# Two-layer diffusion trunk on one core: weight split four units deep, ada loads on the ScalarE queue, a residual scan, and diagonal blocks moved in small pieces

## The reference, cut to what matters

```python
mod = silu(c) @ w_ada + b_ada                       # shift, scale and gate, for latent and context
p = (rmsnorm(x, norm_w) * (1 + sc) + sh) @ w_in     # 2048 -> 8224 columns
# attention: two softmaxes per head, a = p0 - lam * p1
# delta rule, per head and direction, in chunks of C tokens (g cumulated in the chunk):
m = tril_strict(k_beta @ k.T * decay) + eye         # unit triangular
u, w = solve(m, v * beta), solve(m, k_beta * exp(g))
v_new = u - w @ state
o = (q * exp(g)) @ state + (q @ k.T * decay) @ v_new
state = state * exp(g_last) + k_end.T @ v_new
x = x + gt * (concat(y_a, y_b) @ w_out)
```

## Time and profile before

| | us |
|---|---|
| timed runs | 2801.6, 2818.62, 2807.7 |
| median | 2807.7 |
| profiled execution, span from first to last instruction | 2805.5 |
| PE busy | 2441.5 |
| DVE busy | 1479.5 |
| ACT busy | 840.5 |
| POOL busy | 335.5 |

### The profile page before, as it was taken

How to read it: one execution, slowest core, us unless ns; L and a number is a source line. 1 busy time by engine, 2 the same in 40 slices (tenths; PEclk the granted TensorE clock), 3 DMA queues, 4 the chain that set the end, 5 groups by cost and what they waited for, 6 DMA issues and landing times. The chain is left out here.

```text
span 2805.5 us, 41589 instructions
## 1 busy us (share of the span) xinstructions
PE 2441.5 (87%) x15126; PEld 2006.7 (72%) x15126; DVE 1479.5 (53%) x2582; ACT 840.5 (30%) x1415; POOL 335.5 (12%) x685
## 2 busy tenths in 40 slices
PE   6799999999898989897898798988889898987776
PEld 2377778777776868685776476868777686866775
DVE  1345556473737373745433746475656656565535
ACT  3433232323223232323111533223232323223223
POOL 0001011111102020201100002020111202021100
PEclk9999999999999999998998699999999999998888
DMA  8945352626253544434334244443243444333433
GB/s 324 355 113 153 83 152 62 167 70 173 70 152 91 140 104 126 110 102 147 109 104 151 81 108 119 103 107 101 77 110 78 123 106 107 95 92 112 125 110 110
DMA packets 580888, 345.00 MB, mean 123 GB/s; under 512 B 45090, under 2 KB 544966, under 8 KB 579990
## 3 DMA queue, kind: packets, MB, share of 16 engines
q1 hardware_dynamic: 553430, 300.38, 38.7%
q10 hardware_dynamic: 27120, 42.02, 4.7%
q0 software_dynamic: 208, 0.72, 0.1%
HBM read 312.07 MB, written 31.00 MB: 122 GB/s over the span
## 5 line engine op out<-in xcount | busy, mean ns | idle before, releaser
L1604 PE MATMUL ps<-h_hi,w_hi 128*128 128x512 f32 (+1 forms) x2080 | 846.7, 407 | 49.2 <-DVE w_lo L972 38.1
L1605 PE MATMUL ps<-h_lo,w_hi 128*128 128x512 f32 (+1 forms) x2080 | 780.5, 375 | 0.0
L1606 PE MATMUL ps<-h_hi,w_lo 128*128 128x512 f32 (+1 forms) x2080 | 779.6, 375 | 0.0
L972 DVE TENSOR_TENSOR w_lo<-w_raw,w_hi 128x1024 fp32r<-128x1024 f32 (+1 forms) x332 | 405.4, 1222 | 329.7 <-ACT w_hi L569 270.0
L1604 PEld LDWEIGHTS ps<-h_hi,w_hi 128*128 128x128 f32 x2080 | 407.6, 196 | 166.5 <-issue 64.4
L569 ACT CAST w_hi<-w_raw 128x1024 fp32r<-128x1024 f32 (+1 forms) x332 | 340.6, 1029 | 522.0 <-PE ps L1606 197.5
L1606 PEld LDWEIGHTS ps<-h_hi,w_lo 128*128 128x128 f32 x2080 | 407.1, 196 | 70.0
L1605 PEld LDWEIGHTS ps<-h_lo,w_hi 128*128 128x128 f32 x2080 | 409.4, 197 | 47.9
L1457 POOL TENSOR_SCALAR small<-small 128x4 f32<-128x4 f32 (+3 forms) x51 | 14.0, 274 | 2056.5 <-DVE small L1260 1018.1
L1854 PE MATMUL ps<-h_hi,w_hi 128*128 128x512 f32 (+1 forms) x448 | 169.7, 379 | 56.7 <-DVE w_lo L972 56.7
L972 DVE TENSOR_TENSOR arena<-arena,ps 128x512 f32<-128x512 f32 x160 | 104.1, 684 | 129.5 <-PE ps L1686 128.6
(11 more groups left out here) (187 smaller groups left out, 3164.0 us busy)
## 6 DMA issues: line engine op xcount, KB each, us to landing
w_raw<-in_w_in SPq DMA_DIRECT2D x260, 512.0 KB, 4.6
ada_raw<-in_w_ada SPq DMA_DIRECT2D x148, 512.0 KB, 5.4
w_raw<-in_w_out SPq DMA_DIRECT2D x64, 448.0 KB, 3.7
w_raw<-in_w_ada SPq DMA_DIRECT2D x44, 512.0 KB, 7.0
arena<-decay_rows ACTq DMA_DIRECT2D x16, 512.0 KB, 5.4
m_chunks<-arena SPq DMA_DIRECT2D x16, 512.0 KB, 5.5
arena<-s_chunks SPq DMA_DIRECT2D x16, 512.0 KB, 3.9
x_channel_major<-arena ACTq DMA_DIRECT2D x1, 4096.0 KB, 17.2
```

What stands on the lines that cost most here:

```text
L972: return V.tensor_tensor(o, a, b, op)
L1604: mm(o, w_hi[:, s, k], h_hi[:, kt, t0:], start=kt == 0, stop=False)
L1605: mm(o, w_hi[:, s, k], h_lo[:, kt, t0:], start=False, stop=False)
L1606: last = mm(o, w_lo[:, s, k], h_hi[:, kt, t0:], start=False, stop=kt == KT - 1)
```

## The change

It does six things.

- w_raw gets two buffers, w_hi and w_lo four each; the splits run three units ahead (LEAD) instead of one.
- The ada loads inside the heads move from SP's queue to ACT's: after the copy of product k, ACT asks for both halves of k+1; those of k = 0 in slot 30.
- w is not formed any more. From the second step on, PE multiplies the keys by the state (ks_mul), DVE forms the residual v - exp(g) (k state) (residual; the table row is negated once per layer), and v_mul takes one product per direction. POOL no longer forms k_grow, ACT no longer copies w.
- The diagonal blocks move as eight pieces of 16 partitions each way; the DRAM images hold blocks only, and POOL clears inv_T in SBUF instead of a DRAM image of zeros being written once.
- A block of 16 is solved as two halves of 8, both in the same instructions, and joined by two small products on DVE and POOL.
- Slots move: substitution 14 to 17 (was 15 to 19), turns of the inverse 22 and 23 (24, 25), merge levels from 24 (27), v products at 37, 43, 49, 55 (42, 46, 50, 54), output of the head one slot later. The start-up ring of ada loads has seven buffers instead of six.

```diff
+RAW = 2
+SPLIT = 4
+LEAD = SPLIT - 1
+RING = RAW + 5
...
+    def blocks_of(t, b):
+        return t.rearrange("(x b) (r n) -> b r x n", b=NB, n=BLK)[b]
...
-        w_raw = sb("w_raw", [P, 4, HALF, P])
-        w_hi = sb("w_hi", [P, 2, HALF, P], F32R)
-        w_lo = sb("w_lo", [P, 2, HALF, P], F32R)
+        w_raw = sb("w_raw", [P, RAW, HALF, P])
+        w_hi = sb("w_hi", [P, SPLIT, HALF, P], F32R)
+        w_lo = sb("w_lo", [P, SPLIT, HALF, P], F32R)
...
         def substitution(k, d):
+            m, s_ = diagonal_halves(blk_m, d), diagonal_halves(blk_s, d)
+            t = blk_t[d * NT * NB:(d + 1) * NT * NB, 0:2 * SUB * SUB].rearrange("p (h r n) -> p h r n", h=2, r=SUB)
             if d == 0:
-                up = BLK - 1 - k
-                return m[:, 0:up, up:up + 1], s_[:, up:up + 1, up:], s_[:, 0:up, up:], t[:, 0:up, up:]
+                up = SUB - 1 - k
+                return m[:, :, 0:up, up:up+1], s_[:, :, up:up+1, up:], s_[:, :, 0:up, up:], t[:, :, 0:up, up:]
...
+        def corner_product(eng, own, d, out_, a, b):
+            terms = blk_t[d * NT * NB:(d + 1) * NT * NB].rearrange("p (r n k) -> p r n k", r=SUB, n=SUB)
+            own.done(eng.tensor_tensor(terms, a.unsqueeze(2).to_broadcast(terms.shape),
+                                       b.rearrange("p k n -> p n k").unsqueeze(1).to_broadcast(terms.shape), ALU.mult))
+            if d:
+                own.done(eng.tensor_reduce(out_, terms, AX, ALU.add))
+                return
+            for k in (4, 2):
+                own.done(eng.tensor_tensor(terms[:, :, :, 0:k], terms[:, :, :, 0:k], terms[:, :, :, k:2 * k], ALU.add))
+            own.done(eng.tensor_tensor(out_.unsqueeze(3), terms[:, :, :, 0:1], terms[:, :, :, 1:2], ALU.add))
+
+        def join_halves(eng, own, d):
+            i, j = (0, 1) if d == 0 else (1, 0)
+            spare = corner(blk_m, d, j, i)
+            corner_product(eng, own, d, spare, corner(blk_m, d, i, j), corner(blk_s, d, j, j))
+            corner_product(eng, own, d, corner(blk_m, d, i, j), corner(blk_s, d, i, i), spare)
+            own.done(eng.tensor_scalar(corner(blk_s, d, i, j), corner(blk_m, d, i, j), -1.0, None, ALU.mult))
...
+        SUBST, SOLVED, LEVEL0 = 14, 22, 24
+        V_SLOT = (37, 43, 49, 55)
...
             def w_unit(i, u, source, tiles=HALF):
-                s = u % 4
+                s = u % RAW
...
-                    sp.wait_ge(w_split, i * UNITS + (u - 3))
+                    sp.wait_ge(w_split, i * UNITS + (u - RAW + 1))
...
                 def blocks_to_partitions(i):
-                    sp.dma_start(chunk_rows(m_dram), m_T.rearrange("p x c d -> p (x c) d")).then_inc(blocks_out, 16)
-                    sp.wait_ge(blocks_out, nth(layer, i, -1, 16, 16))
-                    sp.dma_start(sub(blk_m), diagonal_blocks(m_dram)).then_inc(blocks_in, 16)
+                    for b in range(NB):
+                        rows = slice(b * BLK, (b + 1) * BLK)
+                        sp.dma_start(blocks_of(m_dram, b),
+                                     m_T.rearrange("p x c d -> p (x c) d")[rows, :, rows]).then_inc(blocks_out, 16)
+                    sp.wait_ge(blocks_out, nth(layer, i, -1, 16 * NB, 16 * NB))
+                    sp.dma_start(blk_m, m_dram).then_inc(blocks_in, 16)
...
-                        if fill and k == 8:
+                        if fill and k == 7:
                             blocks_to_partitions(i)
-                        if fill and k == 10:
+                        if fill and k == 9:
                             blocks_back(i)
...
-                        if k >= 10 and k - 10 < ADA_IN[layer]:
-                            for hf in range(2):
-                                ada_unit(layer, i, k - 10, hf)
...
             def split_hi(i, u, tiles=HALF):
-                s = u % 4
-                act.wait_ge(w_loaded[s], i * (16 * UNITS // 4) + 16 * (u // 4 + 1))
-                need(act, w_used, i * UNITS + (u - 1))
-                nc.scalar.copy(w_hi[:, u % 2, 0:tiles], w_raw[:, s, 0:tiles]).then_inc(w_hi_ready, 1)
+                s = u % RAW
+                act.wait_ge(w_loaded[s], i * (16 * UNITS // RAW) + 16 * (u // RAW + 1))
+                need(act, w_used, i * UNITS + (u - SPLIT + 1))
+                nc.scalar.copy(w_hi[:, u % SPLIT, 0:tiles], w_raw[:, s, 0:tiles]).then_inc(w_hi_ready, 1)
...
                     def ada(k):
                         ada_copy(i * ADA_IN[layer] + (ada_before(layer) + k + 1))
+                        if k + 1 < ADA_IN[layer]:
+                            ada_load(k + 1)
+
+                    def ada_load(k):
+                        lay, firstb = ada_block(layer, k)
+                        for hf in range(2):
+                            act.dma_start(ada_raw[:, hf], w_ada[lay].rearrange("(k p) n -> p k n", p=P)[
+                                :, hf * HALF:(hf + 1) * HALF, bass.ds((i * 2 + (firstb + k % 2)) * P, P)]).then_inc(
+                                    ada_loaded[RAW + hf], 16)
...
                         for j in range(4):
-                            put(42 + 4 * j, v_new_copy, j)
+                            put(V_SLOT[j], v_new_copy, j)
...
+                        put(30, ada_load, 0)
                         for k in range(ADA_IN[layer]):
                             put(43 + 3 * k, ada, k)
...
                         if project and s % 4 == 1:
-                            split_hi(i, base + 2 + s // 4 + 1)
+                            split_hi(i, base + 2 + s // 4 + LEAD)
...
+                    def residual(j):
+                        vec.wait_ge(ks_product, h(-1, 3, j))
+                        for d in range(2):
+                            ch = ORDER[d][j]
+                            m = V.scalar_tensor_tensor(resid[:, d, ch], ps[:, GX[d], 0:P], hcol[:, TAB_GROW, d, ch:ch + 1],
+                                                       v_tok[:, ch], ALU.mult, ALU.add)
...
                     need(pool, s_product, h(-2, 3, 3))
                     for d in range(2):
-                        for n, dst in ((TAB_GROW, k_grow), (TAB_END, k_end)):
...
+                        m = G.tensor_tensor(k_end[:, d], qk_tok[:, NT:], hcol[:, TAB_END, d].unsqueeze(2).to_broadcast([P, NT, P]),
+                                            ALU.mult)
...
+                    G.memset(inv_T, 0.0).then_inc(inv_cleared, 1)
...
-                    def w_mul(d):
...
+                    def ks_mul(j):
+                        pe.wait_ge(s_ready, h(-1, 3, j))
+                        for d in range(2):
+                            ch = ORDER[d][j]
+                            last = mm(ps[:, GX[d], 0:P], qk_T[:, NT + ch], states[:, d, j], start=True, stop=True)
+                        last.then_inc(ks_product, 1)
...
-                            last = mm(ps[:, GT[d], 0:P], inv_T[:, d, ch], v_tok[:, ch], start=True, stop=j == 0)
-                            if j:
-                                last = mm(ps[:, GT[d], 0:P], w_T[:, d, ch], states[:, d, j], start=False, stop=True)
+                            last = mm(ps[:, GT[d], 0:P], inv_T[:, d, ch], resid[:, d, ch] if j else v_tok[:, ch],
+                                      start=True, stop=True)
```

228 lines of the change are left out of this document (112 added, 116 removed).

## The result

The changed kernel takes **2829.6 us** (median of 7 runs, 2821.9 to 2832.4), the kernel before 2810.7 us in the same comparison (7 runs): ratio 1.0065, 95% interval 1.0049 to 1.0081, so it is 18 us slower. The forecast was 2798 us, 10 us faster. The time lies in the range; the sign is wrong.

The account below looks back on a forecast made before the run. It took PE, busy 87% of the span, as the bound; -30 -20 -34 -45 -8 +7 +108 +12 made -10 us, from 2805.5 to 2795.5, with 2.2 us for timed runs 2798 us; range 2745 to 2855 us.

Parts of the forecast that it names:

- the clock's +27: Layer 0 heads: more waiting lowers the granted clock, +4 us a head, +27 us.
- The clock's -15: Output stages: less waiting raises the granted clock, -15 us.
- Part 1: Heads: dropping product w saves PE 30 us (15 to 34); the residual on DVE costs nothing.
- Part 2: Substitution in halves: DVE needs 6.2 us instead of 9.3, shortening PE's wait in layer 0, -20 us (0 to -29).
- Part 3: Weights split three units ahead: w_lo waits go, -34 us in the projections and -45 in the output stages.
- part 4: Layer 1 heads: fewer wide POOL products make DVE's split faster, -8 us (-16 to +8).
- Part 5: Diagonal blocks in eight pieces each way: PE waits for the inverse in layer 1, +7 us (0 to +28).
- Part 6: Ada asked for by ACT in the heads: later asks make PE wait, +108 us (+32 to +185).
- The rival that rests on batching: Small pieces are slow and hold up DVE's turning of the inverse: +64 us at 4 us a head, 2862 us, chance 0.06.
- the w_lo waits: Sign: PE's waits for w_lo fall under 15 us in all.
- the shorter heads of layer 1: Sign: heads of layer 1 become shorter than 124.4 us.
- the 1.4 us at the third tile: Sign: PE waits about 1.4 us at the third score tile, where it waited 4.31 us in layer 0.

Follow-up runs that it names:

- e13: The changed kernel with the scan through w put back (8 products w a head, v slots four apart, no residual on VectorE): 2807.0 us.
- e6: The changed kernel with the substitution of 15 steps on both engines in place of 7 steps and a join: 2820.7 us.
- e5: The changed kernel with four raw and two split weight buffers, asked one unit ahead, as before: 2910.5 us.
- e12: The changed kernel with the blocks carried by one transfer each way, as before, instead of eight pieces: 2834.5 us.
- e3: The kernel before with one edit, ada weights asked for by ACT: 2886.8 us.
- e1_ada_sp: The changed kernel with SP asking for the ada weights again, woven between its weight loads: 2777.9 us.

## Why the prediction was wrong

By its own numbered parts, with the clock's +27 put to ada and -15 to the depth as it had them:

| part | forecast us | measured us | by |
|---|---|---|---|
| 1 product w, residual scan | -30 | +24 | e13 |
| 2 substitution in halves | -20 | +10 | e6 |
| 3 depth | -94 | -80 | e5 |
| 5 small pieces | +7 | -3 | e12 |
| 6 ada on ACT | +135 | +76 | e3 |
| sum (part 4, -8, was not taken alone) | -10 | +27 | 18 measured |

The five measured prices overshoot the result by 9 us, which is within their joint uncertainty. Four were taken in the changed kernel and ada in the kernel before; with the 53 us that e1_ada_sp gives for ada in the changed kernel, where SP's asks stand at other places, the sum would be 4 us. And the agreement is one of the total only. By the profiled executions the prices sum to +71 us in the heads of layer 0 (measured +61), +40 in those of layer 1 (+14) and -82 in the two output stages (-59). So the parts do act on each other, by 20 us and more in a stage, and it cancels. In layer 1 one such effect can be read from the waits: ada on ACT costs 31 us there in the kernel before and 10 in the changed one, where the first multiply of a head waits for VectorE's rotary step anyway (12.2 us of the 19.5) and the ada wait is 22.5 us instead of e3's 36.2.

**Part 1 failed**, in two sentences. "Everything around it is PE work" is why the product was priced at its busy time; in the changed kernel the same products cost 7 us. The likely reason is that PE waits elsewhere in the head for DVE and ada, and a product more is made up there; no run shows it directly. And of the residual it said "so it costs nothing". Its place costs something twice. Moving v to slots 43, 49 and 55 puts ACT's copies of v_new ahead of three ada copies of a head, and the scan's first work on VectorE now stands ahead of the rotary step, which the first ada multiply of a head waits for (19.5 us, in no term of the sum).

How much of the error is part 1's depends on where the copies are booked. Part 6 did see them in slots 43, 49 and 55, and charged them to ada; the kernel before, in which part 6 was measured, has v in slots 42, 46, 50 and 54, with one of three ada copies behind a copy of v_new. With SP asking, the scan saves 12 us instead of costing 24. So in the prediction's own terms part 1 gave -12 us for -30, and part 6, with the 36 us between the two, 112 us for 135. The two errors nearly cancel: together 100 us were measured and 105 forecast. What is left of the wrong sign is then above all part 2 (30 us) and part 3 (14 us), less part 5's 10; part 4's 8 us were not measured.

**Part 2 failed** where it priced the join by DVE alone, and it is the one part with the sign wrong in any booking. 6.2 us were forecast for steps and join; without POOL's join DVE takes 6.2 us of busy time, 6.9 with gaps. Beside it it takes 8.7 us of busy time a head, against 7.9 for the 15 steps before (126.6 us in 16 heads): the part became 0.8 us longer, and nothing came off the third tile's wait. The profile had the row for it, a split at 1.96 us beside POOL's products against 1.22; it was used in part 4 as a gain of fewer wide products and not in part 2, which adds wide products on both engines at the same moment. POOL's own join, 1.7 us of product twice and its sums by adding, was not in the sum at all, and both engines have to be done before the blocks go back.

**Part 3** had nearly the right total and a wrong place. Undoing the depth costs 87 us in the output stages instead of 60, and nothing or less in the heads. (In the whole change these two stages of the table are only 59 us shorter than before; what takes back the other 28 us there, no run shows.) In the heads the w_lo wait was the sign of a late DVE, which the depth cannot make earlier: PE meets it at L1819. In the filled heads of layer 1 PE's wait for w_lo went from 28.1 us to none, and that for the turn of o_a from 9.8 to 39.2 us. The prediction wrote "What is late next is the mix" and named nothing else.

**Part 5**: the pieces overlap as read from the pair of ada loads; the price of 7 us (0 to 28) did not come, since in the changed kernel PE stands before the inverse is wanted (7.2 us at the turned inverse in all). The rival that rests on batching can be dropped.

**Part 6** had the mechanism in each point (late ask, place behind v_new) and an amount too large by 59 us in the kernel before. PE's ada wait in e3_before_ada_act grows by 60 us and its busy time by 17, where 108 and 27 were forecast, and the weight loads, freed of ada, gave nothing back. The term that was too large is the 12.4 us of waiting in a filled head of layer 0: 5.8 us there in e3, 6.9 in the changed kernel, where a pair asked for behind a v_new copy is waited for 2.8 us and not 3.9. In layer 1 it was right, 5.2 us in e3 for a forecast of 5. The clock's part was +27 in the heads of layer 0; there it fell from 0.98 to 0.95 over six heads, but also in layer 1 from 0.96 to 0.92, which was in no term.

That the time fell into the range is in part luck: errors of opposite sign lay in the sum, by the table 84 us too good in parts 1 and 2 and 59 too bad in part 6. Two small slips of its working changed little. The clock's -15 for the output stages comes to -19 by its own factors, and the 33.7 us of product w are already the time in which any of them runs (256 instructions of 274 ns would be 70 us one after another), so no tenth had to come off.

Of the signs under "What would show it", the w_lo waits, the output stages and the longer heads of layer 0 came true; the shorter heads of layer 1 and the 1.4 us at the third tile did not (3.7 to 5.4 us measured, 3.0 to 4.3 before, and about 1.2 without POOL's join). These two were the signs for parts 1, 2 and 3, and they say where the error lay.

## What to carry to other kernels

When two engines are given the same new work at the same moment, price it by a row in which both are busy, and ask which of the two finishes last. A wait on an engine that is simply late moves to the next product that needs it when the first is covered: before you count it as a gain, look whether that engine's work got less. Who asks for a load matters less than what stands ahead of the ask in that engine's order; and where two uses of one buffer stand closer than a load takes, moving the second use can be worth nearly as much as who asks (42 us here for one constant, 53 for the ask).
